# Two or three fp32 products without use, set into the up and down products of the MLP and feed-forward blocks of a six-layer network

## The reference

```python
def sq_relu_mlp(h, w1, w2):                      # w1 1024 x 4096, w2 4096 x 1024, four layers
    return jnp.square(jax.nn.relu(h @ w1)) @ w2

def swiglu(h, w_gate, w_up, w_down):             # 1024 x 2816 twice, 2816 x 1024; four times
    return (jax.nn.silu(h @ w_gate) * (h @ w_up)) @ w_down
```

## Time and profile before

| quantity | value |
|---|---|
| median of 3 runs | 2699.63 us |
| lowest and highest | 2697.34 and 2713.25 us |
| the profiled execution, its own time | 2704.31 us |
| span of the profiled execution | 2702.6 us |
| mean granted clock of PE | 0.993 of full |

### The profile page before, as it was taken

The page is one execution under the profiler, slowest core; times in us unless marked ns, Lnnn a source line. Parts: engine busy times, 40 slices in busy tenths (PEclk is TensorE's granted clock), DMA queues, the critical chain, the costliest instruction groups (busy, mean ns, idle before and its releaser), DMA issues.

```text
span 2702.6 us, 48798 instructions
## 1 busy us (share of the span) xinstructions
PE 2627.6 (97%) x21582; PEld 2555.4 (95%) x21582; DVE 1661.9 (61%) x1970; ACT 1350.9 (50%) x1663; POOL 150.6 (6%) x227
## 2 busy tenths in 40 slices
PE   8989999999999999989999999999999999999998
PEld 8979999899998999988999999989999999999998
DVE  5657655475476754576756665766665657763764
ACT  5645535554436544564545444555444446554543
POOL 3400000000000000330000000000000000000000
PEclk9999999999999999999999999999999999999999
DMA  7514564456544565442565766444766755434663
GB/s 214 164 31 141 189 233 140 145 180 216 201 145 144 173 218 172 145 147 84 175 229 179 199 189 206 141 137 133 194 187 182 197 188 158 140 119 139 187 194 134
DMA packets 429970, 451.96 MB, mean 167 GB/s; under 512 B 13346, under 2 KB 395024, under 8 KB 427584
## 3 DMA queue, kind: packets, MB, share of 16 engines
q1 hardware_dynamic: 417952, 416.12, 49.4%
q0 software_dynamic: 7312, 32.35, 3.5%
q10 hardware_dynamic: 4496, 0.39, 0.1%
HBM read 441.21 MB, written 7.60 MB: 166 GB/s over the span
## 4 chain that ended last, share of the span: by engine, by line
PE 87%; DVE 5%; ACT 4%; POOL 1%; DMA 1%; issue 1%; ACTq 0%; SPq 0%; DVEq 0%
PE ps L602 86%; ACT wH L1463 2%; DVE wL L2088 2%; POOL arena L504 1%; ACT hidden_parts L1523 1%; PE ps L1047 1%; POOL arena L502 0%; DMA arena<-tiles_out 0%; DMA arena<-leaf_out 0%; DVE arena L2626 0%; DMA leaf_out<-arena 0%; POOL arena L512 0%; PE ps L1207 0%; DVE arena L2359 0%; DMA arena<-in_x 0%
## 5 line engine op out<-in xcount | busy, mean ns | idle before, releaser
L2088 DVE TENSOR_TENSOR wL<-ring,wH 128x2048 fp32r<-128x2048 f32 x392 | 898.4, 2292 | 771.9 <-ACT wH L1463 771.5
L1463 ACT ACTIVATE wH<-ring 128x2048 fp32r<-128x2048 f32 x392 | 752.4, 1920 | 1035.9 <-PE ps L602 1034.1
L602 PE MATMUL ps<-hidden_parts,wH 128*128 128x256 f32 x6656 | 1004.3, 279 | 3.8 <-ACT hidden_parts L1523 2.8
L602 PEld LDWEIGHTS ps<-hidden_parts,wH 128*128 128x128 f32 x6656 | 911.5, 189 | 5.8 <-issue 3.6
L602 PE MATMUL ps<-hidden_parts,wL 128*128 128x256 f32 x3328 | 700.2, 279 | 1.4 <-DVE wL L2088 1.4
L602 PEld LDWEIGHTS ps<-hidden_parts,wL 128*128 128x128 f32 x3328 | 524.3, 188 | 1.8 <-DVE wL L2088 1.8
L602 PE MATMUL ps<-hH,wH 128*128 128x256 f32 x2624 | 368.8, 282 | 5.3 <-DVE hH L2105 2.9
L602 PE MATMUL ps<-hH,wL 128*128 128x256 f32 x2624 | 360.2, 279 | 2.2 <-DVE wL L2088 2.2
L602 PE MATMUL ps<-hL,wH 128*128 128x256 f32 x2624 | 347.7, 278 | 0.0
L602 PEld LDWEIGHTS ps<-hH,wH 128*128 128x128 f32 x2624 | 330.3, 189 | 15.3 <-issue 13.5
L602 PEld LDWEIGHTS ps<-hH,wL 128*128 128x128 f32 x2624 | 328.1, 189 | 2.8 <-DVE wL L2088 2.8
(11 more groups left out here) (301 smaller groups left out, 1964.8 us busy)
## 6 DMA issues: line engine op xcount, KB each, us to landing
ring<-in_mlp_w SPq DMA_DIRECT2D x128, 1024.0 KB, 5.4
ring<-in_ffn_w_gate SPq DMA_DIRECT2D x88, 512.0 KB, 4.0
ring<-in_ffn_w_up SPq DMA_DIRECT2D x88, 512.0 KB, 5.3
ring<-in_ffn_w_down SPq DMA_DIRECT2D x44, 1024.0 KB, 5.0
ring<-in_gdn_w_in SPq DMA_DIRECT2D x32, 1024.0 KB, 5.9
ring<-in_w_in SPq DMA_DIRECT2D x28, 1024.0 KB, 5.4
hidden_parts<-mem_parts POOLq DMA_DIRECT2D x14, 1024.0 KB, 7.3
ring<-in_mlstm_w_in SPq DMA_DIRECT2D x12, 1024.0 KB, 5.3
```

The source lines that it names most:

```text
L602: return pe.matmul(o, l, r, start=start, stop=stop, **k)
L1463: f(wH[:, n % PARTS, :], ring[:, n % RING, :], ACT.Copy).then_inc(sem("high_split"), 1)
L2088: tt(wL[:, n % PARTS, :], ring[:, n % RING, :], wH[:, n % PARTS, :].bitcast(F32), ALU.subtract)\
```

## The change

A helper `settle` issues plain fp32 products whose results nobody reads. Its long form (`whole`) has three: 256 columns with the identity as the stationary operand, 128 columns with ones, 128 columns with the identity. Its short form has two of 128 columns, both with the identity. The moving operand is the first chunk of `hT`. Each destination is a half bank of PSUM that is not in use and is overwritten by the next product with its start flag.

The long form stands in each of the four MLP blocks ahead of the second half of up slab 3 (the fourth), and ahead of down slab 4 (the fifth). The short form stands in each of the four feed-forward blocks at the same two places. There the wait for the last four reads of the banks, which used to stand behind the down product, now stands ahead of the short form in the fifth down slab.

```diff
-            def to_channels(name, layer, j, bank, src=(hH, hL), free=None):
+            def to_channels(name, layer, j, bank, src=(hH, hL), free=None, settled=False):
...
                 for m in range(2):
+                    if settled and m == 1:
+                        settle(bank, T, True)
                     last = three(ps[:, bank, m * T:(m + 1) * T],
...
+            def settle(bank, c0, whole):
+
+                x = hT[:, 0, :]
+                if whole:
+                    mm(ps[:, bank, c0:c0 + T], ident, x, True, True)
+                    mm(ps[:, bank, c0 + P:c0 + T], ones[:, 0:P], x[:, 0:P], True, True)
+                else:
+                    mm(ps[:, bank, c0:c0 + P], ident, x[:, 0:P], True, True)
+                mm(ps[:, bank, c0:c0 + P], ident, x[:, 0:P], True, True)
...
-            def down_product(name, layer, chunks, waited, at_third=None, end_by_pairs=False):
+            def down_product(name, layer, chunks, waited, at_third=None, end_by_pairs=False, at_fifth=None):
...
+                    if at_fifth and j == 4:
+                        at_fifth()
...
-                    to_channels("mlp_w1", i, j, bank_of(j), free="bank_read")
+                    to_channels("mlp_w1", i, j, bank_of(j), free="bank_read", settled=j == 3)
...
-                down_product("mlp_w2", i, 32, range(0, 32, 2), floor, end_by_pairs=True)
+                down_product("mlp_w2", i, 32, range(0, 32, 2), floor, end_by_pairs=True,
+                             at_fifth=lambda: settle(4, 0, True))
...
                     for half in range(2):
+                        if n == 3 and half == 1:
+                            settle(4 + n % 4, T, False)
                         last = three(ps[:, 4 + n % 4, half * T:(half + 1) * T],
...
-                down_product(f"{kind}_w_down_2", l, 22, range(22))
-                pe.wait_ge(sem("bank_read"), W.next("bank_read", 4))
+
+                def settled():
+                    pe.wait_ge(sem("bank_read"), W.next("bank_read", 4))
+                    settle(4, 0, False)
+
+                down_product(f"{kind}_w_down_2", l, 22, range(22), at_fifth=settled)
```

## The result

| | before | after |
|---|---|---|
| median of 14 runs each | 2699.64 us | 2718.0 us |
| lowest and highest | 2689.93, 2715.71 | 2712.63, 2724.83 |
| the profiled execution | 2704.31 us | 2724.3 us |

The ratio is 1.0071 with a 95% interval of 1.0054 to 1.0088: the change costs 0.7%, some 18 us. The forecast was 2691 us and a gain.

The account below looks back on a forecast made before the run. PE was taken as the bound, by its entries times the distance between starts. 2704.3 + 10.7 price - 20.2 gained pace = 2694.8 us profiled, less the 4.7 us to the median: 2690, given as 2691 us, range 2682 to 2714.

Parts of the forecast that it names:

- The pace as what matters: In long product stretches PE has two paces at one clock, 113.2 and 117.6 ns per entry, 4.4 ns apart.
- The price: Eight long forms in the MLPs, 7.1 us, and eight short ones in the feed-forward blocks, 3.6 us: 10.7 us.
- The moved wait: Four bank reads awaited ahead of the fifth down slab: costed at nothing, at most one DVE bank read if late.
- The pace behind the long form: In the MLPs, the long form leaves PE fast, as the decays do; 1370 slow products in the third become fast.
- the eight pairs: Pairs or parts of pairs of decays in the two delta-rule mixers; what follows them was fast in all eight.
- The pace behind the short form: In the feed-forward blocks, the short form leaves PE fast, with less confidence; 2832 and 336 slow products become fast.
- The mechanism: The pace is a phase between loads and products, set by the last irregular moment and kept; gain 20.2 us.
- Rival 3: Both forms leave PE slow; 3826 fast MLP products become slow too, 17.0 us: 2738 us; chance 0.04.
- Rival 1: The short form leaves PE slow: MLPs gain 6.1 us, feed-forward blocks lose 10.7 us, 2715 us; chance 0.14.
- Rival 2: The pace isn't set by what is issued, so the cost stands alone: 2710 us; chance 0.12.

Follow-up runs that it names:

- The catalogue: Thirteen forms of fp32 products, rotated over some 190 places in the up and down slabs of all eight blocks, against the kernel before; 2858.3 us.
- the table of six points: Threes in up slabs: one 128-column product, the long form, the long form again behind 0 to 5 extra fp32r products; no time given.

## Why the prediction was wrong

**The pace as what matters: right.** In the eight blocks the loss is the pace and the price. What else differs between the two profiled executions, waits and clock ahead of and between the blocks, is the 9.6 us of chance above.

**The price: right.** 10.7 us forecast; 0.91 us for a long form and 0.46 to 0.48 for a short one in the trace. The moved wait cost nothing.

**The pace behind the long form: wrong.** I took one long form for "one `decay` call" and carried over what follows the decays. But those eight places show two calls in a row each. Doubled, the form does what I said (15 of 16 places); single, it gives 0 of 8. The rows were thin as well: seven of the eight pairs came in fast already. The one that came in slow came in late (220 ns), and from a late entry the single long form is fast too, 28 times of 28. In the changed kernel seven long forms came in even and one fast. The forecast had the MLPs 1.0 us slower (7.1 of price less 6.1 gained in the third). Measured, they lost 3.9 + 8.1 + 1.8 + 8.1 = 21.9 us.

**The pace behind the short form: wrong.** "I take fast, by the nearest in operands and type." It was slow at six of eight. I had put the two outcomes in the earlier trace rows down to which operand the weights are. The catalogue has eight narrow products from fast to slow (9 places) and from slow to fast (7) with the weights as the stationary operand each time, and two narrow ones likewise (13 and 2): I had left out the pace at entry. Three of the eight short forms came in fast, which is always slow behind. The forecast had the feed-forward blocks 10.5 us faster (3.6 of price less 14.1 gained); they lost 8.0.

**Which of the two turned the sign?** Either would have. The MLPs missed their forecast by 21 us and the feed-forward blocks by 19, against a forecast gain of 9.5. The 9.6 us of chance outside the blocks hide a quarter of that.

**The mechanism: right, but with a wrong conclusion.** "Each is such an irregular moment, of always the same form. Its value is the pace in which PE comes out." A form has no such value by itself. It maps the phase at entry to one at exit, and that depends on its widths, their number and, at a late entry, the tensor read. From one observed outcome of one form nothing follows for another. That the pace is "a phase between the loads and the products" fits the loads: 110 ns from load to product in the fast pace, 114 or 115 in the slow one. Whether the long third load is the cause of the slow pace or its sign, no run shows.

**The rivals.** Rival 3, both forms slow, came closest in kind; I gave it 0.04 and 2738 us. It was too high because the short form was fast at two places, the first MLP's end turned fast in its wait, and the profiled execution of the change was 9.6 us shorter outside the blocks. The chance was too low: the evidence against it was the eight pairs alone. Rivals 1 and 2 gave 2715 and 2710 us, nearer to the 2718, but that is luck. Rival 1 has the long forms gain 6.1 us. Rival 2, a pace not set by what is issued, is refuted for the pace behind a form by the table of six points; what breaks a pace between two forms it may still describe.

By the Trainium skill (TensorE: Matmul & The Clock Gate, "Wait — 56ns, not 53.3ns?") a product takes at full clock its columns by 2.4 GHz plus some 2.5 ns, an estimated 109 ns for 256 columns. No long stretch here shows that: the fast pace is 113 and the slow one 117.5 ns at granted clock 1.00.

## What to carry to other kernels

When a trace shows two paces for the same products at one clock, count the entries of each stretch before explaining anything by waits; a few nanoseconds over ten thousand products are 1 to 2% of a kernel. To steer the pace, copy a form only whole (number, widths, operands and the pace at entry), or try a dozen forms in one kernel, each followed by a slab that shows the outcome, and sort them by the pace at entry. Blocks change their pace from one execution to the next as well, so compare medians of many runs.

## What the runs showed of the hardware

- fp32r products of 128x256 run at 113.3 or 117.8 ns from start to start at the full clock, for more than a thousand in a row. A block's wait can throw it from one to the other. So can a single late start: 36 and 73 ns late did it in one kernel, 35 and 30 ns late did not.
- The slow pace has a period of three products: every third weight load lasts 192 ns instead of 187 or 188. The long form entered at one third of it comes out fast (28 of 28), at the two others slow (51 of 51).
- Which tensor a useless product reads changes the outcome at late entries: one narrow product is fast at 4 of 4 with hT and at 0 of 9 with a constant, two are fast at 0 of 3 with hT and at 2 of 2 with a constant. These are few places. Why is open. The address, its place beside the identity in one tensor, or what else is read at the time were not told apart.
- The spread of the kernel's own times may come in part from this. With one product at 16 places eight runs lie within 5.3 us, where 19 of before lie within 20.5 us on that chip. On another chip nine of ten runs of the same kernel lie within 4.8 us, but the tenth is 11.5 us above them.
- Why a start is late in the third down slab of the feed-forward blocks, with no wait that the profile names, is open too.
